# Hybrid decoder layer on one core: first units split by chunk pairs, zero matmuls in a gap, first block evacuated ahead of conversions, small loads on another queue

## The reference

```python
h = rmsnorm(x, g_mix)
proj = h @ w_in                       # 1024 x 4608: q, k, v (512 each), u (1024), two gates (1024 each)
o = moba_attention(q, k, v)           # 8 heads of 64; one block of 256, so causal softmax
z = a * sigmoid(g)                    # u + b_glu split in a, g
z = causal depthwise conv of 31 taps; layernorm; silu
merged = gate_a * (o @ w_attn_up) + gate_c * (z @ w_conv_pw + b_conv_pw)
x = x + merged @ w_out
x = x + square(relu(rmsnorm(x, g_ffn) @ w_ff1)) @ w_ff2
return rmsnorm(x, g_final)
```

## Time and profile before

| | |
|---|---|
| median of 3 runs | 362.22 us |
| profiled execution | 362.36 us |
| its span in the trace | 360.4 us |
| PE busy | 349.6 us (97%) |
| DVE busy | 253.2 us (70%) |
| ACT busy | 183.9 us (51%) |
| granted TensorE clock | 0.995 of full |
| read from and written to HBM | 62.48 and 1.05 MB |

### The profile page before, as it was taken

The page is one execution under the profiler, slowest core; times in us unless marked ns, Lnnn a source line. Parts: engine busy times, 40 slices in busy tenths (PEclk is TensorE's granted clock), DMA queues, the critical chain, the costliest instruction groups (busy, mean ns, idle before and its releaser), DMA issues.

```text
span 360.4 us, 4567 instructions
## 1 busy us (share of the span) xinstructions
PE 349.6 (97%) x1736; PEld 287.0 (80%) x1736; DVE 253.2 (70%) x302; ACT 183.9 (51%) x219; POOL 10.6 (3%) x18
## 2 busy tenths in 40 slices
PE   6899999999999999999999999999999999999993
PEld 3678888777777888888888888888888888888882
DVE  1779999899989589983848754638546384563834
ACT  3695645577796564444635634416354163551413
POOL 3000000000005000000000000000000000000000
PEclk9999999999999999999999999999999999999997
DMA  7999464533335653855364483762738537260003
GB/s 266 342 354 329 124 228 140 210 118 116 118 116 203 207 199 119 251 167 199 126 225 130 158 296 118 240 225 75 276 115 256 209 106 249 110 233 0 0 0 116
DMA packets 33993, 63.71 MB, mean 177 GB/s; under 512 B 1178, under 2 KB 5434, under 8 KB 33980
## 3 DMA queue, kind: packets, MB, share of 16 engines
q1 hardware_dynamic: 33676, 63.01, 52.1%
q10 hardware_dynamic: 304, 0.53, 0.4%
HBM read 62.48 MB, written 1.05 MB: 176 GB/s over the span
## 4 chain that ended last, share of the span: by engine, by line
PE 90%; ACT 2%; DMA 2%; issue 2%; SPq 2%; DVE 0%; POOLq 0%; POOL 0%; ACTq 0%
PE ps L828 20%; PE ps L832 19%; PE ps L829 19%; PE ps L1023 17%; PE ps L1025 8%; PE ps L815 3%; DMA raw<-in_w_in_dram 2%; PE ps L886 1%; ACT w_hi L391 1%; SPq L301 1%; PE ps L914 1%; SPq L316 1%; PE ps L889 0%; ACT nat L410 0%; ACT nat L428 0%
## 5 line engine op out<-in xcount | busy, mean ns | idle before, releaser
L828 PE MATMUL ps<-w_hi,a_lo 128*128 128x512 f32 x288 | 114.0, 396 | 3.0 <-DVE a_lo L601 1.9
L832 PE MATMUL ps<-w_lo,a_hi 128*128 128x512 f32 x288 | 112.6, 391 | 0.3 <-DVE w_lo L606 0.3
L829 PE MATMUL ps<-w_hi,a_hi 128*128 128x512 f32 x288 | 112.3, 390 | 0.0
L1023 PE MATMUL ps<-b_both,w_hi 128*128 128x512 f32 x256 | 90.8, 399 | 0.0
L1025 PE MATMUL ps<-b_both,w_lo 128*128 128x256 f32 x256 | 72.0, 281 | 0.0
L589 DVE TENSOR_TENSOR w_lo<-raw,w_hi 128x2048 fp32r<-128x2048 f32 x29 | 66.1, 2286 | 6.4 <-ACT w_hi L391 6.3
L391 ACT CAST w_hi<-raw 128x2048 fp32r<-128x2048 f32 (+1 forms) x30 | 56.4, 1882 | 24.9 <-PE ps L832 21.0
L779 DVE TENSOR_TENSOR w_lo<-raw,w_hi 128x2048 fp32r<-128x2048 f32 x28 | 63.5, 2289 | 6.4 <-ACT w_hi L563 6.4
L828 PEld LDWEIGHTS ps<-w_hi,a_lo 128*128 128x128 f32 x288 | 54.2, 188 | 15.1 <-DVE w_hi L595 2.1
L832 PEld LDWEIGHTS ps<-w_lo,a_hi 128*128 128x128 f32 x288 | 54.1, 188 | 12.3 <-DVE w_lo L606 0.8
L829 PEld LDWEIGHTS ps<-w_hi,a_hi 128*128 128x128 f32 x288 | 54.2, 188 | 10.6
(11 more groups left out here) (111 smaller groups left out, 218.5 us busy)
## 6 DMA issues: line engine op xcount, KB each, us to landing
raw<-in_w_ff_dram SPq DMA_DIRECT2D x32, 1024.0 KB, 5.5
raw<-in_w_in_dram SPq DMA_DIRECT2D x14, 1024.0 KB, 5.1
raw<-in_w_out_dram SPq DMA_DIRECT2D x4, 1024.0 KB, 5.1
raw<-in_w_in_dram SPq DMA_DIRECT2D x6, 512.0 KB, 7.9
raw<-in_w_attn_up_dram SPq DMA_DIRECT2D x2, 1024.0 KB, 5.0
raw<-in_w_conv_pw_dram SPq DMA_DIRECT2D x2, 1024.0 KB, 5.0
res<-in_x_dram SPq DMA_DIRECT2D x2, 512.0 KB, 4.2
raw<-in_w_in_dram SPq DMA_DIRECT2D x4, 256.0 KB, 5.5
```

The lines of the kernel that those rows point to most:

```text
L828: nc.tensor.matmul(dst, lo[:, tok], w_hi[:, slot, k], start=start, stop=False)
L829: nc.tensor.matmul(dst, hi[:, tok], w_hi[:, slot, k], start=False, stop=False)
L832: return nc.tensor.matmul(dst, hi[:, tok], w_lo[:, slot, k], start=False, stop=stop)
L1023: nc.tensor.matmul(ps[:, TB + c], w_hi[:, slot, k, cols], b_both[:, kk].rearrange("p a t -> p (a t)"), start=kk == 0, stop=False)
```

## The change

It has four parts.

1. Units 0, 1 and 2 are each loaded in two chunk pairs, with semaphores `first_*`, `second_*`, `third_*` for the first pair. Of unit 0's first pair, DVE makes the high half of chunk 0 and ACT that of chunk 1; the first pairs of units 1 and 2 are made high by ACT, low by DVE (`low_pair`), each between the pairs of x chunks. PE takes units 0 and 1 by pairs of chunks: first all products with `w_hi` (`high_products`), then those with `w_lo` (`low_products`), each behind its own wait; the number of matmuls is the same. Unit 2 waits for all its halves. The two squares of x move between these conversions.
2. Five more zero matmuls (`WARM_AGAIN`) behind the x transposes.
3. `take(0)` moves from the end of ACT's step 1 to its front, ahead of the copies of `vec` and `dw`, and `high(3)` moves from step 0 to behind them; `high(4)` follows. In steps 2 and 4 `high(n + 3)` moves from the front of the step to behind the GLU part, that is behind `conv_first`.
4. The six small loads are issued by ACT, behind the first sigmoid and ahead of the g_mix copy.

```diff
@@ SP
             load_halves(0, slice(0, 2), first_full)
             load_halves(0, slice(2, HK), raw_full[0])
-            for n in range(1, U_LOOP):
+            load_halves(1, slice(0, 2), second_full)
+            load_halves(1, slice(2, HK), raw_full[1])
+            load_halves(2, slice(0, 2), third_full)
+            load_halves(2, slice(2, HK), raw_full[2])
+            for n in range(3, U_LOOP):
...
-                if n == 1:
-                    for row, v in ((V_BGLU, b_glu), ...
-                        sp.dma_start(o_t[row:row + rows, 0, 0:P], ...).then_inc(vec_full, 16)
-                    sp.dma_start(dw_rows, ...).then_inc(vec_full, 16)
@@ ACT
-                part = slice(0, HK) if n else slice(2, HK)
+                part = slice(0, HK) if n > 2 else slice(2, HK)
...
             nc.scalar.activation(first_sig[:], zero_b[:, 0:1], ACT.Sigmoid)
+            for row, v in ((V_BGLU, b_glu), ...
+                act.dma_start(o_t[row:row + rows, 0, 0:P], ...).then_inc(vec_full, 16)
+            act.dma_start(dw_rows, ...).then_inc(vec_full, 16)
...
                 if pair == 1:
+                    act.wait_ge(first_full, 32)
+                    nc.scalar.copy(w_hi[:, 0, 1], raw[:, 0, 1]).then_inc(first_hi[1], 1)
+                    act.wait_ge(x_full[0], 16)
+                    square_input(0)
                     high(0)
+                if pair == 2:
+                    act.wait_ge(second_full, 32)
+                    nc.scalar.copy(w_hi[:, 1, 0:2], raw[:, 1, 0:2]).then_inc(second_hi, 1)
             high(1)
+            act.wait_ge(third_full, 32)
+            nc.scalar.copy(w_hi[:, 2, 0:2], raw[:, 2, 0:2]).then_inc(third_hi, 1)
+            act.wait_ge(x_full[1], 16)
+            square_input(1)
             high(2)
...
             for n in range(U_LOOP):
-                if n + AHEAD < U_LOOP + AHEAD_LOOP:
-                    high(n + AHEAD)
                 if n == S_VEC:
+                    take(0)
                     act.wait_ge(vec_tr, 1)
...
+                    high(AHEAD)
+                if n and n + AHEAD < U_LOOP + AHEAD_LOOP and n not in GLU_AT:
+                    high(n + AHEAD)
                 if n in GLU_AT:
...
+                if n in GLU_AT:
+                    high(n + AHEAD)
...
-                if n < U_ATTN and n % 2 == 1 and n // 2 < GA:
+                if n < U_ATTN and n % 2 == 1 and 0 < n // 2 < GA:
                     take(n // 2)
@@ DVE
-            dve.wait_ge(first_full, 32)
-            nc.vector.tensor_copy(w_hi[:, 0, 0:2], raw[:, 0, 0:2]).then_inc(first_hi, 1)
...
+                    if k == 0:
+                        dve.wait_ge(first_full, 32)
+                        nc.vector.tensor_copy(w_hi[:, 0, 0], raw[:, 0, 0]).then_inc(first_hi[0], 1)
                 if pair == 0:
+                    dve.wait_ge(first_hi[0], 1)
+                    dve.wait_ge(first_hi[1], 1)
+                    low_pair(0, 0, first_lo)
                 if pair == 1:
                     dve.wait_ge(hi_made, 1)
+                    low_pair(0, 1, lo_made)
+                if pair == 2:
+                    dve.wait_ge(second_hi, 1)
+                    low_pair(1, 0, second_lo)
+                if pair == 3:
+                    dve.wait_ge(hi_made, 2)
+                    low_pair(1, 1, lo_made)
-            low(1)
-            low(2)
+            dve.wait_ge(third_hi, 1)
+            low_pair(2, 0, third_lo)
             dve.wait_ge(sq_made, TT)
             nc.vector.tensor_scalar(ms[:, 0], sq_sum[:, 0, 0:TT], ...).then_inc(ms_made, 1)
+            dve.wait_ge(hi_made, 3)
+            low_pair(2, 1, lo_made)
@@ PE
+            for _ in range(WARM_AGAIN):
+                nc.tensor.matmul(ps[:, 0], zero_b[:, 0:P], zero_b[:], start=True, stop=True)
...
+            for k in (0, 1):
+                pe.wait_ge(xt_lo, k + 1)
+                pe.wait_ge(first_hi[k], 1)
+                high_products(0, k)
+            pe.wait_ge(first_lo, 1)
+            for k in (0, 1):
+                low_products(0, k)
+            pe.wait_ge(xt_lo, 4)
+            pe.wait_ge(hi_made, 1)
+            for k in (2, 3):
+                high_products(0, k)
+            pe.wait_ge(lo_made, 1)
+            for k in (2, 3):
+                last = low_products(0, k)
+            last.then_inc(used, 1)
...
+            pe.wait_ge(xt_lo, 6)
+            pe.wait_ge(second_hi, 1)
...
+                if n == 2:
+                    pe.wait_ge(third_lo, 1)
```

More of the change, by code:

```diff
@@ L26 @@
 WARM = 9
+WARM_AGAIN = 5
 AHEAD = 3
@@ L203, in build @@
         first_full = sem("first_full")
-        first_hi = sem("first_hi")
+        first_hi = [sem(f"first_hi{k}") for k in range(2)]
         first_lo = sem("first_lo")
+        second_full = sem("second_full")
+        second_hi = sem("second_hi")
+        second_lo = sem("second_lo")
+        third_full = sem("third_full")
+        third_hi = sem("third_hi")
+        third_lo = sem("third_lo")
         gmix_full = sem("gmix_full")
@@ L395, in _, with square_input @@
             nc.scalar.activation(first_sig[:], zero_b[:, 0:1], ACT.Sigmoid)
+            for row, v in ((V_BGLU, b_glu), (V_BDW, b_dw), (V_LNG, ln_g), (V_LNB, ln_b), (V_GFFN, g_ffn)):
+                rows = v.shape[1] // P
+                act.dma_start(o_t[row:row + rows, 0, 0:P], v.rearrange("l (c p) -> (l c) p", p=P)).then_inc(vec_full, 16)
+            act.dma_start(dw_rows, w_dw.rearrange("l j (c p) -> (l j c) p", p=P)).then_inc(vec_full, 16)
+            def square_input(t):
+                nc.scalar.activation(nat[:, t], res[:, t], ACT.Square, accum_out=sq_sum[:, 0, t:t + 1]).then_inc(sq_made, 1)
             act.wait_ge(gmix_tr, 1)
@@ L404, in _ @@
                 if pair == 1:
+                    act.wait_ge(first_full, 32)
+                    nc.scalar.copy(w_hi[:, 0, 1], raw[:, 0, 1]).then_inc(first_hi[1], 1)
+                    act.wait_ge(x_full[0], 16)
+                    square_input(0)
                     high(0)
+                if pair == 2:
+                    act.wait_ge(second_full, 32)
+                    nc.scalar.copy(w_hi[:, 1, 0:2], raw[:, 1, 0:2]).then_inc(second_hi, 1)
             high(1)
+            act.wait_ge(third_full, 32)
+            nc.scalar.copy(w_hi[:, 2, 0:2], raw[:, 2, 0:2]).then_inc(third_hi, 1)
+            act.wait_ge(x_full[1], 16)
+            square_input(1)
             high(2)
-            for t in range(TT):
-                nc.scalar.activation(nat[:, t], res[:, t], ACT.Square, accum_out=sq_sum[:, 0, t:t + 1]).then_inc(sq_made, 1)
             def take(b):
@@ L592, in _, with low_pair @@
             nc.vector.memset(zero_b[:], 0.0).then_inc(zero_made, 1)
-            dve.wait_ge(first_full, 32)
-            nc.vector.tensor_copy(w_hi[:, 0, 0:2], raw[:, 0, 0:2]).then_inc(first_hi, 1)
+            def low_pair(n, pair, made):
+                part = slice(2 * pair, 2 * pair + 2)
+                nc.vector.tensor_tensor(w_lo[:, n, part], raw[:, n, part], w_hi[:, n, part].bitcast(F32),
+                                        ALU.subtract).then_inc(made, 1)
             dve.wait_ge(gmix_made, 1)
@@ L822, in transpose_chunks, with products @@
                 return last
-            def products(slot, k, hi, lo, bank, t, start, stop, low_sem=None):
+            def products(slot, k, hi, lo, bank, t, start, stop):
                 dst = ps[:, bank]
@@ L866, in _ @@
                         last.then_inc(x_tr, 1)
[L869 to L875, removed]
-                for t in range(TT):
-                    last = products(0, k, a_hi[:, k], a_lo[:, k], t, t, k == 0, False,
-                                    first_lo if k == 0 and t == 0 else None)
+            for _ in range(WARM_AGAIN):
+                nc.tensor.matmul(ps[:, 0], zero_b[:, 0:P], zero_b[:], start=True, stop=True)
@@ new lines, in high_products, with low_products @@
+            def high_products(n, k):
+                for t in range(TT):
+                    tok = slice(t * P, t * P + P)
+                    nc.tensor.matmul(ps[:, t], a_lo[:, HK * n + k, tok], w_hi[:, n, k], start=n == 0 and k == 0, stop=False)
+                    nc.tensor.matmul(ps[:, t], a_hi[:, HK * n + k, tok], w_hi[:, n, k], start=False, stop=False)
+            def low_products(n, k):
+                for t in range(TT):
+                    tok = slice(t * P, t * P + P)
+                    last = nc.tensor.matmul(ps[:, t], a_hi[:, HK * n + k, tok], w_lo[:, n, k], start=False,
+                                            stop=n == 1 and k == HK - 1)
+                return last
@@ new lines, in _ @@
+            last.then_inc(used, 1)
+            pe.wait_ge(xt_lo, 6)
+            pe.wait_ge(second_hi, 1)
+            for k in (0, 1):
+                high_products(1, k)
+            pe.wait_ge(second_lo, 1)
+            for k in (0, 1):
+                low_products(1, k)
+            pe.wait_ge(xt_lo, KD)
+            pe.wait_ge(hi_made, 2)
+            for k in (2, 3):
+                high_products(1, k)
```

(12 more changed lines are left out.)

7 lines of the change are left out of this document (removed).

## The result

The changed kernel takes 366.67 us (median of 4 runs, 366.37 to 367.07), the kernel before 362.34 in the same session: the ratio is 1.0118 (95% interval 1.0105 to 1.0132), so it is slower, by 4.3 us. The profiled execution took 366.37 us, its span is 364.6, PE is busy for 353.5 us in it, DVE for 253.0, ACT for 184.0.

The account below looks back on a forecast made before the run. PE bounds the kernel (90% of the chain). The 3.0 us early gain is lost; DVE, 5.2 late less 1.69 slack, delays unit 14 by 3.5: 362.36 + 3.5 = 365.9, forecast 365.8 us, range 363.0 to 367.6.

Parts of the forecast that it names:

- The wait in front of the two low halves: DVE waits for ACT's copy before low(5) and low(7), near 2.7 us each, making them 2.4 and 5.2 us late.
- The slack of 1.69 us, taken once: At attention step 0's row maximum, DVE's only wait absorbs 1.69 of the 5.2 us, leaving it 3.5 late.
- Unit 14 takes the full delay: PE's unit 14 has no slack, so DVE's 3.5 us delay reaches it: 103.59 becomes 107.1, nothing given back.
- The start: Units 0 and 1 run dense, GLU transposes no longer wait, take(0) at 19.6: early gain of 3.0 us.
- the first product: PE's first product of unit 0 starts at 8.45 against 9.19, thanks to halved conversions.
- The clock: Rival: half clock behind PE's new stall loses 1.9 us, nearly whole hidden; about 367; chance 0.12 shared with wrong start.
- The small loads and the zeros: Six issues on ACT free from 2.89 on; five zero matmuls end at 8.4, gain nothing; no time taken for either.
- The early gain is kept: Rival: DVE not held or its spare time takes the delay, early 3.0 us partly reach unit 14; 359.4 at best; chance 0.11.
- Half the delay: Rival: idle in softmax steps between row maximum and unit 14 closes 2.8 of the 3.5 us: 363.1; chance 0.07.
- The start goes wrong as well: Rival: slow zero matmuls (+1.0) or dearer ACT issues (up to +2.7) ahead of take(0): 366.9 to 368.6; 0.12 with clock.

Follow-up runs that it names:

- e3: Kernel before, with only the high halves of units 5 and 7 moved behind conv_first in ACT's steps 2 and 4: 365.45 us, ratio 1.0091.
- e1: Changed kernel with the high halves of units 5 and 7 at the front of ACT's steps 2 and 4 again: 360.68 us, ratio 0.9953.
- e8: Changed kernel with only unit 7's high half at the front of step 4 again, unit 5's still behind conv_first: 363.50 us, ratio 1.0024.
- e4: Changed kernel with new ACT order: high(3) ahead of take(0), high(4) behind vec and dw, high(5) and high(7) between sigmoids and conv_first: 359.64 us.
- e5: Changed kernel without the five second zero matmuls (WARM_AGAIN) behind the x transposes: 366.35 us, ratio 1.0106.
- e7: Changed kernel with sixteen zero matmuls in PE's stall in front of the second scores (step 10): 365.84 us, ratio 1.0093.
- e9: The changed kernel itself, timed once more on another occasion: 366.43 us, ratio 1.0103.
- e11: The kernel of e4 with the six small loads on SyncE's queue besides: 359.70 us, ratio 0.9922 to the kernel before.
- e2: Changed kernel with ACT's whole order of steps 0 to 4 as before the change: 362.25 us, ratio 1.0012.
- e10: The kernel of e6 again, timed beside the changed kernel: 365.97 us, ratio 1.0101 to the kernel before.
- e6: Changed kernel with the six small loads on SyncE's queue again, behind unit 1's loads: 365.74 us, ratio 1.0092.

## Why the prediction was right, and where it was off

*The wait in front of the two low halves.* Right in place and size: 2.75 us twice, forecast as 2.8. The low half of unit 5 was put at 31.1 and came at 31.63, that of unit 7 at 46.4 and came at 46.79. e3 shows that this edit alone loses 3.3 us, e1 that without it the rest gains 1.5.

*The slack of 1.69 us, taken once.* Right: the row maximum was put at 75.3, is at 75.62 and has no wait. e8 shows the arithmetic with one hole: forecast 363.6, measured 363.50. The slack also explains two numbers that the prediction didn't have. In e1 the gain stops at 1.5 us, because PE's lead takes away DVE's wait of 1.69, and from there on DVE is late itself (z is no earlier than before, 28.98 against 27.81). And the two holes cost 3.3 us in the kernel before, which still has the slack, but 6.0 in the changed kernel (366.67 against e1's 360.68), where it is spent: 2 x 2.75 and up to 0.6 for the clock.

*Unit 14 takes the full delay.* Right in its mechanism: 3.83 at the row maximum is 4.16 at unit 14, and nothing of the last 260 us gives it back.

*The start.* The first units run without a gap as said, and the zero matmuls took 1.24 us for five, as at the fast pitch. The term that was mis-sized is the first product: 8.45 forecast, 9.04 in the trace. Of these 0.59 us, 0.43 lie in front of the first a_hi, at 7.13 and not at 6.70. x was not late: its second load landed 4.5 us behind its issue, before the change 4.7. The transposes of x were slow: the first three are 0.42 to 0.48 us long, where before only the first is longer than 0.27 (0.33). The prediction took TensorE's fast pitch to be there by 5.3, as in the one execution that it had read; here it came about half a microsecond later. What set this isn't shown: the granted clock reads 1.00 from the first zero matmul on, although these run at the slow pitch. The other 0.16 is the way from the first a_hi to the first product, 1.91 us here (1.91 or 1.92 in e4, e5, e7, e9 and e11) and 1.75 in the prediction's sum. In e1, e2 and e10 the landing of the first weights comes on top, which the prediction took for fixed too.

Through take(0) at 20.26 (forecast 19.6) this made z 0.6 late. It did not pass to the end one for one, as the prediction said such a slip would: the row maximum is only 0.3 late, since from z to the low half it takes 3.62 us and not 3.73, twice, and 28.83 from low(7) to the row maximum and not 28.9.

*The clock.* This rival was held to hide nearly whole. The stall (3.60 us, forecast 3.6) did lower the clock, which agrees with the rule of the Trainium skill that the prediction named (TensorE: Matmul & The Clock Gate, "Why this matters for your kernels"). Its price for PE was sized well, 1.9 us forecast and 2.0 measured against e7 and e3. It showed all the same, because PE stood later than the prediction had it: not 1.1 but 1.45 behind the old schedule at the second scores, and 0.7 more by the small waits. That makes 4.18 at the third scores, 0.35 more than the 3.83 of DVE's chain, and unit 14 is 4.16 late.

So unit 14 came at 107.75 in place of 107.1: 0.3 from the start and 0.35 from the clock. The rest of the 0.9 us between the forecast (365.8) and the measured 366.67 is within the scatter of the runs (366.37 to 367.07). That the number came so near is in part luck, as the late start and the short way from z to the low halves have opposite signs.

*The small loads and the zeros.* Nothing was added for them, and the times show nothing. The issues cost 0.29 to 0.37 us each, as supposed. They did not wait for the sigmoid.

*The rivals.* "The early gain is kept" had 0.11 and did not happen; it takes another order on ACT, as in e1 and e4. "Half the delay" by closing idle time on the way did not happen. "The start goes wrong as well" named zero matmuls at the slow pitch or dear issues; neither came, and the start was late by another way.

## What to carry to other kernels

Before a piece of work is moved on one engine's list, ask what the next engine does in that place: here ACT was idle for 2.5 us until z was made, with the next weights ready, and DVE, full for 40 us, had to wait 2.75 behind it. A lead of 2 to 3 us on the bounding engine is worth only as much as the slack of the engines that it meets later; find that slack (one bracket in a timeline, 1.69 us) and hold every new delay against it. An edit in several parts can hide a gain under a loss: reversing the two lines made 366.67 into 360.68.

## What the runs showed of the hardware

ACT's queue issues DMAs while its engine is busy: these rows of the changed kernel's ACT timeline stand beside a table load that lasts from 1.40 to 2.68, where the prediction had them start at 2.89, behind the sigmoid.

```profile
1.40 1.28 ACT L401 ACT_TABLE_LOAD   x1 [1.40 <-PEq L1154]
1.47 0.29 ACTq L404 DMA_DIRECT2D o_t<-in_b_glu_dram  x1
1.79 0.31 ACTq L404 DMA_DIRECT2D o_t<-in_b_dw_dram  x1
```

Four of the six issues start before the table load has ended, and so ahead of the sigmoid (2.69).

The granted clock fell in the stalls of 3.60 us (changed kernel, e5) and 3.59 (e9), and behind those of 3.63 and 3.62 (e6 and e10: the first four score matmuls still took 0.70 us, the six transposes after the scores 1.54 where they take 0.82 to 0.88 at full clock), and not behind that of 1.16 (e8) or when zero matmuls filled it (e7).
